# Expert weighting in a decoder layer: diagonal tiles written by VectorE in place of ScalarE

## The reference

```python
def peer_block(xb, w_query, sub_keys, u_tab, v_tab):          # xb: 128 rows of 1024
    q = (xb @ w_query).reshape(T, PEER_HEADS, 2, PEER_DK // 2)
    s = jnp.einsum('thcd,hcnd->thcn', q, sub_keys)
    s1, i1 = lax.top_k(s[:, :, 0], 16); s2, i2 = lax.top_k(s[:, :, 1], 16)
    ...                                                        # the 16 best of the 256 sums, e: their experts
    gate = jax.nn.softmax(top_s, axis=-1)
    act = jax.nn.gelu(jnp.einsum('thkd,td->thk', u_tab[e], xb))
    return jnp.einsum('thk,thkd->td', gate * act, v_tab[e])
```

## Time and profile before

| | us |
|---|---|
| median of three runs | 3503.95 |
| the three runs | 3503.14, 3503.95, 3511.46 |
| the profiled execution | 3511.46 |
| its span, first to last instruction | 3509.3 |

### The profile page before, as it was taken

One profiled execution on the slowest core, in us unless ns is written; L12 is line 12 of the kernel. 1 busy time (PEld: TensorE's weight loads), 2 busy tenths in 40 slices (PEclk: granted clock), 3 DMA queues, 4 the chain that ended last, 5 costly groups with the idle time before them and its releaser, 6 DMA issues.

```text
span 3509.3 us, 53126 instructions
## 1 busy us (share of the span) xinstructions
PE 2804.1 (80%) x19302; PEld 1383.5 (39%) x19302; DVE 2522.2 (72%) x5894; ACT 1435.5 (41%) x3859; POOL 1371.8 (39%) x1199
## 2 busy tenths in 40 slices
PE   8999977777778767976797779787878787777657
PEld 4555565434344324432443334334433344323211
DVE  2477333878877877788778877887788777776774
ACT  2121122535533553356335633574357433333332
POOL 0000000443454345434543454345444545454452
PEclk9999988988879888889888888898989888878879
DMA  3122343999999999999999999999999999999998
GB/s 99 40 58 82 107 144 130 403 415 401 410 413 414 395 419 415 404 403 418 416 405 408 415 415 405 396 418 416 403 406 412 417 414 410 401 416 399 409 419 343
DMA packets 248373, 1237.82 MB, mean 353 GB/s; under 512 B 62816, under 2 KB 90384, under 8 KB 112560
## 3 DMA queue, kind: packets, MB, share of 16 engines
q0 software_dynamic: 160256, 1132.54, 79.0%
q1 hardware_dynamic: 87856, 101.90, 8.6%
HBM read 1210.82 MB, written 23.53 MB: 352 GB/s over the span
## 4 chain that ended last, share of the span: by engine, by line
DMA 30%; PE 22%; DVE 20%; ACT 7%; issue 5%; POOL 1%; ACTq 0%; SPq 0%; DVEq 0%; POOLq 0%
DMA uv_ring<-in_peer_uv,expert 30%; PE peer_y L2464 11%; DVE uv_ring L1769 9%; PE peer_s L2020 3%; PE beside L2056 2%; PE scan L2144 2%; ACT diag L1996 1%; ACT L1985 1%; DVE same L1380 1%; DVE same L1382 1%; DVE pick L1384 1%; POOL uv_ring L1336 1%; ACT weights L1989 1%; ACT gelu L1985 1%; ACT L1941 1%
## 5 line engine op out<-in xcount | busy, mean ns | idle before, releaser
L1336 POOL DMA_INDIRECT uv_ring<-in_peer_uv,expert x1056 | 1223.6, 1159 | 1631.3 <-PE peer_y L2464 1282.4
L2464 PE MATMUL peer_y<-uv_ring,diag 64*64 64x512 f32 x8192 | 1250.3, 735 | 574.8 <-ACT diag L1996 541.9
L1769 DVE CUSTOM_DVE_ANT_0 uv_ring<-uv_ring,p_h 128x1024 f32<-128x1024 f32 x1056 | 1270.3, 1222 | 469.7 <-DMA uv_ring<-in_peer_uv,expert 463.5
L2464 PEld LDWEIGHTS peer_y<-uv_ring,diag 64*64 64x64 f32 x8192 | 307.9, 153 | 1181.6 <-ACT diag L1996 795.5
L1985 ACT ACTIVATE gelu<-hidden 128x2 f32<-128x2 f32 x528 | 107.4, 203 | 1420.6 <-DVE hidden L1769 1419.4
L594 PE MATMUL proj<-mix,w_in_tile 128*128 128x512 f32 x672 | 296.7, 600 | 0.0
L1996 ACT ACTIVATE diag<-ident_halves,weights 128x64 f32<-128x64 f32 x1024 | 292.5, 332 | 0.0
L1989 ACT ACTIVATE weights<-gelu,p_gate 128x1 f32<-128x1 f32 x1056 | 254.1, 287 | 50.5 <-ACT gelu L1985 1.5
L2020 PE MATMUL peer_s<-wk,p_h2t 128*128 128x256 f32 x1024 | 252.4, 402 | 4.0 <-DVE cand L1361 4.0
L2020 PEld LDWEIGHTS peer_s<-wk,p_h2t 128*128 128x128 f32 x1024 | 199.9, 201 | 96.4 <-issue 46.2
L1985 ACT ACT_TABLE_LOAD x172 | 220.7, 1283 | 3.0
(11 more groups left out here) (453 smaller groups left out, 3746.3 us busy)
## 6 DMA issues: line engine op xcount, KB each, us to landing
uv_ring<-in_peer_uv,expert POOLq DMA_INDIRECT x1056
w_in_tile<-in_w_in SPq DMA_DIRECT2D x24, 512.0 KB, 3.3
w_out_rows<-in_w_out SPq DMA_DIRECT2D x24, 512.0 KB
uv_ring<-in_w_query SPq DMA_DIRECT2D x8, 1024.0 KB, 7.0
scan_in<-scratch_scan_in SPq DMA_DIRECT2D x15, 480.0 KB, 8.5
pages_ring<-scratch_k_tiles SPq DMA_DIRECT2D x36, 192.0 KB, 12.5
pages_ring<-out_v_new SPq DMA_DIRECT2D x36, 192.0 KB, 11.4
p_x<-in_x_rows SPq DMA_DIRECT2D x9, 512.0 KB, 8.7
```

Source lines behind the costliest of these rows:

```text
L1336: pool.indirect_dma_start(out=uv_row(m), out_offset=None, in_=io["peer_uv"], in_offset=bass.IndirectOffsetOnAxis(ap=expert[:, t % 4, k:k + ...
L1769: nc.vector.tensor_tensor_reduce(out=u_row(m), in0=u_row(m), in1=h2[:, b % 2, :], scale=1.0, scalar=0.0, op0=ALU.mult, op1=ALU.add, accum_ ...
L2464: ins = nc.tensor.matmul(Y[r][rows[j], :], diag[rows[r], m % DIAGS, :], v_row(m, rows[r], slice(j * 512, (j + 1) * 512)), start=begin, sto ...
```

## The change

ScalarE's two kinds of small instruction, the gate product and the diagonal tile, go away with the tile `weights` and its semaphore. VectorE gets `weigh(t, q)`: for each of the two picks one `tensor_scalar` that multiplies the identity by the gelu and by the gate, each a value per partition, into `diag`. It stands in each step behind the choice piece and ahead of `beside`. VectorE waits there for the gelu of the same step, and for `uv_free` as ScalarE did. ScalarE's gelu waits for the diagonals of two steps back, since they read `gelu`.

```diff
@@ vector
+            def weigh(t, q):
+
+                b, h = divmod(t, PH)
+                g = at_group(t, q)
+                dve.wait_ge(gelu_done, g + 1)
+                dve.wait_ge(G.sem, G.at("gate", t))
+                eye, n = (ident4, NS) if last(b) else (ident2, HT)
+                for k in range(GP):
+                    m = g * GP + k
+                    if m >= DIAGS:
+                        dve.wait_ge(uv_free, m - DIAGS + 1)
+                    nc.vector.tensor_scalar(diag[:, m % DIAGS, 0:n], eye[:, 0:n], gel[:, g % 2, k:k + 1], gate[:, t % 4, q * GP + k:q * GP + k + 1],
+                                            ALU.mult, ALU.mult).then_inc(diag_done, 1)
...
                     if later_turn < TURNS:
                         choose(later_turn, piece)
+                    weigh(t, q)
                     if b and h == 0 and q == 0:
                         add_values(b - 1)
@@ scalar
                     act.wait_ge(dotted, GP * (g + 1))
+                    if g >= 2:
+                        act.wait_ge(diag_done, GP * (g - 1))
                     nc.scalar.activation(gel[:, g % 2, :], hid[:, g % 2, :], ACT.Gelu_apprx_tanh).then_inc(gelu_done, 1)
-                    act.wait_ge(G.sem, G.at("gate", t))
-                    act.wait_ge(gelu_done, g + 1)
-                    for k in range(GP):
-                        nc.scalar.activation(wgt[:, g % 2, k:k + 1], gel[:, g % 2, k:k + 1], ACT.Copy,
-                                             scale=gate[:, t % 4, q * GP + k:q * GP + k + 1]).then_inc(weights_done, 1)
-                    for k in range(GP):
-                        m = g * GP + k
-                        act.wait_ge(weights_done, m + 1)
-                        if m >= DIAGS:
-                            act.wait_ge(uv_free, m - DIAGS + 1)
-                        nc.scalar.activation(diag[:, m % DIAGS, 0:n], eye[:, 0:n], ACT.Copy, scale=wgt[:, g % 2, k:k + 1]).then_inc(diag_done, 1)
```

5 lines of the change are left out of this document (2 added, 3 removed).

## The result

The changed kernel takes 3557.47 us (median of four runs, 3553.78 to 3575.91) beside 3504.31 us for the kernel before. The ratio is 1.0157, with the interval 1.012 to 1.0196: slower by 53 us by the medians (55 by the ratio). The forecast was slower by 23 us, with a range that ended at 3556. The profiled execution took 3559.5 us, its span is 3557.7 us.

A forecast was written before the change was run, and what follows sets the result against it. Gather streaming bounds the expert stage, VectorE five heavy turns. Each gets 3.6 + 0.8 + 0.5 + 1.0 = 5.9 us, less about 1; with leftovers and tail +24 us: forecast 3527 us, range 3501 to 3556.

The forecast's parts named there:

- What VectorE gets: VectorE's 1056 new TENSOR_SCALAR in the expert stage: about 0.45 us a pair, 3.6 us per turn of eight pairs.
- The five turns: Sixth turns of blocks 1 to 5, 41.72 to 43.42 us each, taken as bound by VectorE; to grow to 46 or 47.
- the leftovers of the other turns: Turns outside the heavy five: 5.9 us barely fit VectorE's idle 5.3 and 5.9 us; 2 us put for the rest.
- the cushion: Queue of gathers absorbing VectorE's lateness: about 1 us of each heavy turn's 5.9; possible span 0 to 3 us a turn.
- The new wait: VectorE waiting for the same step's gelu: 0.8 us per heavy turn in even steps, about 0.5 in a late odd step.
- A rule weighed: POOL's gather issue holding one in four of VectorE's new instructions by 0.26 us: 1.0 us per turn.
- The worse direction: VectorE keeping POOL from writing descriptors, so DMA runs dry; under B, 0.31 us at each gather, 25 us more, 3552.
- What moves for TensorE: Diagonals 0.5 us earlier in even steps; last step's slot 2.7 us later, covered outside the heavy turns, not added inside.
- A: Whole expert stage: DMA is the bound and VectorE has 22% idle, so nothing moves: 3504 us; chance 0.25.
- B: Slower in all turns: VectorE blocks on gelus delayed through TensorE by later diagonals; 3575, or 3543 with a third; chance 0.15.
- C: Faster: slots back 0.5 us earlier in four of eight steps, gain bounded by 11.7 us: 3492; chance 0.05.

The follow-up runs named there:

- work: Kernel before, with VectorE also writing two unread scratch tiles per step behind the choice piece; ScalarE still makes the diagonals: 3531.83 us against 3508.97, ratio 1.0069.
- heavy: Changed kernel with VectorE writing diagonals only in the sixth turn of blocks 1 to 5, ScalarE elsewhere: 3517.44 us, before 3507.49, ratio 1.0036.
- wait: Kernel before, with VectorE waiting for the step's gelu behind the choice piece and no instruction more: 3514.57 us against 3508.97, ratio 1.0019.
- twoin: Changed kernel with SCALAR_TENSOR_TENSOR in place of TENSOR_SCALAR, the gate broadcast as a second tensor: 3564.42 us, ratio to the kernel before 1.0165.
- odd: Changed kernel with VectorE writing diagonals only in odd steps (those with a choice piece), ScalarE in the others: 3559.16 us, before 3507.49, ratio 1.0154.
- early: Changed kernel with VectorE's diagonals directly behind the dots in every step, ahead of gates and choice piece: 3645.62 us, before 3508.97, ratio 1.0384.
- late: Kernel before, with ScalarE writing the diagonals of odd steps only after VectorE's choice piece is done: 3533.14 us against 3508.97, ratio 1.0077.
- seven: Changed kernel with VectorE writing diagonals only in the last step of each turn, ScalarE in the others: 3521.47 us, before 3507.16, ratio 1.0046.
- ring6: Kernel before with 6 ring slots in place of 7: 3636.9 us against 3506.78, ratio 1.0378.
- even: Changed kernel with VectorE writing diagonals only in even steps (no choice piece), ScalarE in the others: 3509.42 us, before 3507.49, ratio 1.0007.
- single: Kernel before, with ScalarE doing gelu, weight and diagonal pick by pick as each dot product is out: 3496.29 us against 3506.78, ratio 0.9972.
- lateodd: Kernel before, with ScalarE's odd-step diagonals held until the choice piece is done and VectorE's two scratch tiles in odd steps: 3544.26 us against 3507.16, ratio 1.0112.
- evensingle: Changed kernel with VectorE making diagonals in even steps, ScalarE pick by pick in odd steps: 3543.69 us, before 3506.78, ratio 1.011.

## Why the prediction was right or wrong

**What VectorE gets: right in the sum.** The forecast took 225 to 310 ns apiece and some near 570; the trace has 301, 314 and 557 ns as shortest, median and longest. The five turns were to grow to 46 or 47 us under 380 GB/s: they take 46.4 us at 368 to 378. As a price in time, the two terms for VectorE's own work, 3.6 + 1.0 us in five turns, with the leftovers of the other turns and less the cushion, come to 18 us; work measured 24, of which its trace puts 15 into the five turns. VectorE's idle time before dots fell below 300 us and ScalarE's share to 26%, as forecast. But nearly all of the forecast's sum, 22.9 of 24 us, lay in the five turns with everything that burdens them, and heavy, which has just that, costs 10 to 13 us. The forecast left out that the turn behind a slow one is shorter; that work alone comes out near the forecast of 23 is in part luck.

**The new wait: right.** 0.8 + 0.5 us in five turns is 6.5 us; wait measured 7, and in its trace the five turns grow by 10 us and the turns behind them shrink by 4. The 69.3 us over 203 waits in the changed profile are more than that; where in the program they cost nothing was not followed.

**A rule weighed: right in the size of the hold, and worth nothing that shows.** The longest instructions took 0.24 us more than the median, where the forecast had 0.26. A third were held and not a quarter, most of them for less: the 1024 durations have a mean of 354 ns over a median of 314, 41 us in sum, which is 0.6 us a turn where the forecast had 1.0. The direction is the one that the third instruction in the earlier trace rows showed, and the one that the Trainium skill, "SBUF — State Buffer", section "Who interferes with whom", gives for such a pair; here the trace agrees. But twoin takes the holds away and the time stays. The 1.0 us a turn for them should have been left out, or the number of instructions on VectorE been seen as what counts; which of the two, the runs do not tell. The worse direction of the section "SBUF: two separate sides" of the same page of the Trainium skill, VectorE keeping POOL from its descriptors, does not show as a cause: POOL's issues take 1191 ns in the mean in the changed kernel, 32 more than the 1159 of the kernel before, but odd loses 54 us with 1168 ns, and early, which loses most of all, has 1124.

**What moves for TensorE: the step that failed.** The forecast worked out that the diagonals of the last step end 4.0 us after the dots and the slot comes back 2.7 us later. Then it said: "Outside the five turns the queue of gathers covers this." The reason given was that a slot lives 17.5 us and the compute part of that is a few us. The reason does not carry: if a slot is in use for 17.5 us at full rate and there are just seven, then every us that the compute part takes longer is taken from the time in which the gather is on its way. late shows 27 us for the lateness alone, without any work on VectorE; seven shows 14 to 16 us for the last step alone; ring6 shows that no slot is spare. With this term at 27 instead of 0, the sum of 23 would have been 50 us, beside the 53 measured. That this comes so near is in part luck: late delays the slots more than the change does, and by the table the changed kernel's own lateness is worth some 12 us, which leaves 12 open. The delay itself, 2.7 us in the last step and next to nothing behind the score product, was forecast right; its price was not.

**The cushion.** It was taken from the earlier trace rows, in which VectorE idles 5.3 and 5.9 us for gathers, and called the softest term. That idle time tells that VectorE is not the bound; it does not tell that a late slot is free. In the profile before this could be read: of POOL's 1631 us of waiting most is for the matmuls that free a slot, 587 times in 528 steps, so nearly every step's gathers are issued at the moment a slot comes back, and a slot 1 us later is a gather 1 us later. The forecast named that wait and then said that it costs nothing while enough gathers are queued. By ring6, late and seven a quarter to a third of such a delay ends up in the time.

**The rivals.** A (hidden) is out with a loss of 53 us. B had the right region, 3543 to 3575, and as its first mechanism later diagonals that hold ScalarE's gelu by way of TensorE's part; what was found is nearer to its general sense (a loss outside the five turns, by lateness) than to its mechanism, which no run isolated. Its sign, every turn longer by 1 us or more, is not met: in block 0 the turns grow by 0.6 to 3.7 us, elsewhere some shrink. Its price by missing VectorE time is not borne out, and neither is the one by holds of POOL. C (faster, since even steps come 0.5 us earlier) did happen in its place: even is +2 us although it carries half of VectorE's new work, worth 12 us if it scales with the 24 of work. Its slots come 0.2 to 0.9 us earlier than before, and the earlier diagonals seem to give about 10 us back; this is by subtraction and was not isolated, but single gains 10 us by nothing but earlier diagonals, which speaks for it.

**Open.** odd is 15 us above lateodd and a part of the 7 us of wait explains only some of it; their intervals, added up, reach about 14 us. It is of the size of the 12 us that the changed kernel's sum leaves open, and what both are was not found. The 23 us of blocks 0 and 6 are more than work, wait and late have there together. How the changed kernel's loss divides over the turns between work and lateness cannot be read off, since the turns behind a slow one catch up (heavy).

## What to carry to other kernels

Where a queue of buffers is refilled the moment one comes free, ask of each moved instruction when it now releases a buffer. Here slots that came 0.6 us later in the mean cost 27 us, as much as all the new instructions (late and work), and that the engine which got them had "22% idle" foretold neither. A DMA busy share of 1.0 is not full rate: compare the GB/s of stretches. The engine that waits for free slots says whether a delay is passed on, and one slot less is a cheap way to measure how much of it. The same work is free in a step where nothing stands between it and what feeds it, dear behind a long piece of other work, and dearer ahead of that piece, where the engine waits for its feeder with all the rest queued behind; try the places apart before judging the engine that does it. And look where the table loads are after any edit to ScalarE's waits.

## What the runs showed of the hardware

- The DMA share stayed between 0.98 and 1.01 over stretches of 343 us and more whose rate went from 393 to 412 GB/s, with the number of gathers on the way and the time at which they start (the kernel before, the changed one, ring6, single). Over single turns the rate went down to 368 GB/s at a share of 0.94.
- TENSOR_SCALAR over 128x64 with two scalars took 314 ns, or up to 557 beside POOL's instructions (all 342 above 340 ns had one beside them); SCALAR_TENSOR_TENSOR over the same tile took 281 ns and never above 352. The second is shorter and steadier, and the kernel is not faster by it.
- A ring of six slots in place of seven cost 130 us where a slot's life unchanged would have cost some 480 (estimate): from issue to issue a slot lived 17.0 us in place of 19.1.
- ScalarE's table load, 1.28 us, ran ahead of the wait for the dots in the kernel before, the changed kernel and even, and behind it in 73 of 81 cases in the even steps of evensingle and in 74 of 172 in single.
- In single each of a step's two gelus of 128x1 took 200 ns, and one of 128x2 took 203 ns in the changed kernel: splitting so small an instruction costs its whole length again. ScalarE was busy 48% of the span by it, and the kernel was 10 us faster.
